# First attention of a two-block transformer forward pass: pairs of heads interleaved as two difference pairs and one MoBA pair, twice per token tile

## The chip, the cores and the metric

The kernel runs on one core of one Trainium2 chip. The metric is the time of one execution on the device in microseconds (us), the median of three runs. Engines are named as in the profile: PE is TensorE (PEld its weight loads), DVE is VectorE, ACT is ScalarE, POOL is GpSimd, SP is SyncE, whose queue fetches the weights.

## The reference

Two small transformer blocks run one after the other over 256 tokens of width 1024, in float32. The change lies in the very first mixer, which computes two kinds of attention from one projection `h = x @ w_in`:

```
def diff_moba_mixer(x, w_in, lam, subln, w_out, lambda_init, rope_d, rope_m):
    h = x @ w_in
    ...
    a = diff_attention(dq, dk, dv, lam, subln, lambda_init)
    b = moba_attention(mq, mk, mv)
    return jnp.concatenate([merge_heads(a), merge_heads(b)], axis=-1) @ w_out
```

Difference attention has 4 heads. Each has two query and key maps of width 64 and one value of width 128; both maps go through a causal softmax and the output weights are `w = p[0] - lam_full * p[1]`. A head's output is then normalized by its root mean square over 128 values and scaled by `subln`. MoBA attention has 4 heads of width 128; with 256 tokens and a block of 256 it comes down to plain causal softmax attention over the one block. Afterwards come layer norms, a squared-ReLU MLP, a gated linear attention, another MLP, and the second block with grouped attention, cross attention, pooling and gated convolutional FFNs.

## The kernel before

Each engine has its own program, written out by hand, and the programs meet only at semaphores. Tokens are handled in two tiles t of 128. Weights come as 207 slabs of 1 MB through a ring of six buffers; ScalarE makes the high part `wh` of a slab (line 586), VectorE the rest `wl` (line 1004), and TensorE multiplies three products of high and low parts.

In the first attention the work is cut into 12 steps, the list `HY_PAIRS` (lines 364 to 366). A step ("pair") is either `("diff", t, h)`, one difference head, whose two maps fill the two halves of a score bank, or `("moba", t, j)`, two MoBA heads. Both put 2 x 128(t+1) scores into one PSUM bank. In the order before, a tile has its four difference pairs first and then its two MoBA pairs. All engines walk through this list in its order:

- TensorE (`attention`, line 2001): for step k it issues the scores of pair k+2 (`scores`, 1920: a bf16 mask matmul on line 1927, then the products on line 1929 for a difference pair and 1939 for a MoBA pair), the transposes of the probabilities of pair k (`probs_T`, 1950, line 1968), and the product with the values of pair k-1 (`values`, 1971, line 1998). Scores of the first two pairs are issued earlier, inside the last chunk of the input projection. The transposes of a difference pair wait for VectorE's `diff_w`, those of a MoBA pair for ScalarE's `exp_done` alone.
- VectorE (`softmax`, 1156): for pair q it takes the maximum of the scores (line 1186) and the scaled bias `nb` (1192), then the after-work `post` of pair q-1. For a difference pair that is a reciprocal, a scaling of the second map and the difference (1165, 1167, 1169). For a MoBA pair it is the copy of the transposed probabilities from PSUM (1178), which waits for `pT_ready`. Behind these, `beside_hy` (1387) puts in, at fixed places, the sums of squares of the first tile's difference heads (k = 4, line 1376), its MoBA output (k = 5, lines 1370 and 1206) and its difference output (k = 7, lines 1383 and 1385), each three pairs after the pair of that number.
- ScalarE (`softmax`, 662): for pair q the two exponentials with row sums (683), then, where pair q-1 is a difference pair, the copy of its transposed weights (672). With pair 6 it also squares the first tile's difference outputs (`diff_squares`, 809, line 811); the squares of the second tile stand behind the loop, and behind them one weight split (line 586) and then the copies of `prep("hy_out")` (593).

The squares of a tile read the PSUM bank that holds all four difference heads of that tile, so `diff_squares(t)` waits on `pv_done`, the count of finished value products, for the last difference pair of the tile. The difference heads of tile 0 go to bank 5, of tile 1 to bank 7; the MoBA heads of both go to bank 6, which the second tile may use once `moba_free` is signalled. Score banks rotate over three, banks for transposes over two.

When the last value product is done, TensorE transposes the first tile of `xn` (line 1646), ScalarE and VectorE make its high and low parts `xhl` (593 and 1017), and the output projection begins (`project_out`, 1685, lines 1706 to 1708). The second tile of `xn` is transposed in the middle of it.

Of the kernel before, what the change touches and what calls it, by code (L numbers as in the profile page):

```python
# [161 lines left out]
def build(nc, d):  # L162
    st, S = plan()
    out = d["out"]
    with ExitStack() as ctx:
# [3 lines left out]
        def sem(name):  # L169
            return ctx.enter_context(nc.semaphore(name))  # L170
# [52 lines left out]
        def ar(col, *dims):  # L223

            n = int(np.prod(dims))
            v = arena[:, col:col + n]
            if len(dims) == 2:
                v = v.rearrange("p (a b) -> p a b", b=dims[1])
            elif len(dims) == 3:
                v = v.rearrange("p (a b c) -> p a b c", b=dims[1], c=dims[2])  # L230
            return v
# [87 lines left out]
        pv_done = sem("pv_done")  # L319
# [43 lines left out]

        HY_PAIRS = []
        for t in range(TT):
            HY_PAIRS += [("diff", t, h) for h in range(4)] + [("moba", t, j) for j in range(2)]
        QK_PAIRS = [("gqa", t, j) for t in range(TT) for j in range(4)]
        XA_PAIRS = [("x", t, j) for j in range(2) for t in range(TT)]
        Q_HY, Q_QK = 0, len(HY_PAIRS)
# [36 lines left out]
        def out_bank(kind, t, j):  # L406

            if kind == "diff":
                return 5 if t == 0 else 7
            if kind == "moba":  # L410
                return 6
            if kind == "gqa":
                return 6 + j // 2
            return 4 + 2 * t + j
# [156 lines left out]
        def _(act):  # L571
# [235 lines left out]
            blocks(0, HY_FILLS, fs=(4, 6))  # L807

            def diff_squares(t):
                act.wait_ge(pv_done, Q_HY + 6 * t + 4)  # L810
                nc.scalar.activation(ar(HY_SQ, TT, CH)[:, t, :], ps[out_bank("diff", t, 0)][:, :], ACT.Square).then_inc(sq_done, 1)

            softmax(HY_PAIRS, Q_HY, lambda k: diff_squares(0) if k == 6 else None, lambda k: copy_nat(5) if k == 1 else None)
            diff_squares(1)
            splits(st["hy_out"], 0, 1)
            prep("hy_out")
# [1544 lines left out]
```

## Time and profile before

| | |
|---|---|
| runs | 1339.33, 1339.55, 1338.05 us; median 1339.33 |
| profiled execution | 1339.7 us |
| its span | 1337.7 us |
| mean granted TensorE clock | 0.996 of full speed |
| busy, share of the span | PE 97%, PEld 84%, DVE 68%, ACT 51%, POOL 7% |
| first attention, first pair's maximum to the output projection's first matmul | 79.22 to 110.35 us |

The span is what the profiler saw from first to last instruction; the time of that execution is 2.0 us longer. A busy share is an average over the whole kernel; in the first attention TensorE is far less busy than 97%. In the timelines a line is one instruction or several alike in a row (the count after x); the end of a TensorE line is modelled and overlaps the next one, so what a matmul costs in a row is read from start to start. The granted clock is 1.00 at 2.4 GHz and 0.50 at 1.2 GHz.

### The profile page before, as it was taken

The page shows a single profiled execution, that of the slowest core. Times are in us where ns is not written, and L with a number is a line of the kernel's source. Part 1 is how long each engine was busy: PE and PEld are TensorE (multiplying, and loading weights), DVE is VectorE, ACT ScalarE, POOL GpSimd, SP SyncE. Part 2 cuts the span into 40 slices and gives each one's busy share as a digit, 9 for nine tenths or more (in the row PEclk, how much of TensorE's full clock was granted, in tenths as well). Part 3 has the DMA queues.
Part 4 walks back from the last instruction along what each step waited for, and adds up shares of the span by engine and source line. Part 5 has one row for each costly group of instructions (what it writes and reads, how often), then busy time and mean ns, then how long its engine had stood idle before and what let it go on. Part 6 is the DMA issues. An engine that isn't in the chain of part 4 may idle for free.

```text
span 1337.7 us, 18077 instructions
## 1 busy us (share of the span) xinstructions
PE 1303.3 (97%) x7247; PEld 1124.6 (84%) x7247; DVE 912.0 (68%) x997; ACT 683.1 (51%) x817; POOL 98.3 (7%) x135
## 2 busy tenths in 40 slices
PE   8989999999999999999999999999999989999997
PEld 6867888888888888888888888888888888788885
DVE  4987766657477865666777655787777545687776
ACT  5653544445644454444646543566665442566663
POOL 3100100001240100000220100000001100000000
PEclk9999999999999999999999999999999999999999
DMA  9722655556443655554650533555557441455540
GB/s 347 288 95 82 235 194 192 188 189 216 170 132 129 219 197 192 194 193 167 250 177 11 219 128 126 186 193 192 191 192 246 158 152 56 173 194 194 193 168 31
DMA packets 36066, 235.57 MB, mean 176 GB/s; under 512 B 4136, under 2 KB 4512, under 8 KB 10016
## 3 DMA queue, kind: packets, MB, share of 16 engines
q1 hardware_dynamic: 30384, 217.07, 45.2%
q0 software_dynamic: 4608, 15.82, 3.7%
q10 hardware_dynamic: 1008, 1.77, 0.4%
q8 instruction: 46, 0.75, 0.2%
q14 instruction: 20, 0.16, 0.0%
HBM read 232.54 MB, written 2.10 MB: 175 GB/s over the span
## 4 chain that ended last, share of the span: by engine, by line
PE 85%; DVE 8%; ACT 3%; DMA 2%; issue 1%; POOL 1%; SPq 0%; POOLq 0%; ACTq 0%; DVEq 0%
PE ps L1799 20%; PE ps L1793 11%; PE ps L1814 7%; PE ps L1816 7%; PE ps L1815 7%; PE ps L1706 3%; PE ps L1708 3%; PE ps L1707 3%; PE ps L1676 2%; PE ps L1678 2%; PE ps L1677 2%; DVE wl L1004 2%; PE ps L1998 2%; PE ps L1772 2%; PE ps L1777 2%; PE ps L1773 2%
## 5 line engine op out<-in xcount | busy, mean ns | idle before, releaser
L1004 DVE TENSOR_TENSOR wl<-raw,wh 128x2048 fp32r<-128x2048 f32 x203 | 463.1, 2289 | 169.8 <-ACT wh L586 169.6
L586 ACT ACTIVATE wh<-raw 128x2048 fp32r<-128x2048 f32 x203 | 386.7, 1908 | 139.1 <-PE ps L1799 77.0
L1799 PE MATMUL ps<-xhl,wh 128*128 128x512 f32 x1216 | 290.1, 391 | 0.0
L1799 PEld LDWEIGHTS ps<-xhl,wh 128*128 128x128 f32 x1216 | 223.5, 188 | 43.2
L1814 PE MATMUL ps<-wh,hh 128*128 128x512 f32 x432 | 168.3, 390 | 2.8 <-DVE hl L1291 2.8
L1815 PE MATMUL ps<-wl,hh 128*128 128x512 f32 x432 | 168.1, 389 | 0.0
L1816 PE MATMUL ps<-wh,hl 128*128 128x512 f32 x432 | 168.1, 389 | 0.0
L1793 PEld LDWEIGHTS ps<-xhl,wl 128*128 128x128 f32 x1216 | 155.9, 191 | 6.0 <-issue 0.6
L1793 PE MATMUL ps<-xhl,wl 128*128 128x256 f32 x1216 | 159.0, 284 | 0.0
L1814 PEld LDWEIGHTS ps<-wh,hh 128*128 128x128 f32 x432 | 81.1, 188 | 20.4 <-DVE hl L1291 3.7
L1816 PEld LDWEIGHTS ps<-wh,hl 128*128 128x128 f32 x432 | 81.1, 188 | 16.9
L1815 PEld LDWEIGHTS ps<-wl,hh 128*128 128x128 f32 x432 | 81.1, 188 | 16.8
L1676 PE MATMUL ps<-wh,xhl 128*128 128x512 f32 x208 | 82.4, 396 | 0.4 <-DVE xhl L1017 0.2
L1677 PE MATMUL ps<-wl,xhl 128*128 128x512 f32 x208 | 81.1, 390 | 0.0
L1678 PE MATMUL ps<-wh,xhl 128*128 128x512 f32 x208 | 81.0, 390 | 0.0
L1269 DVE SCALAR_TENSOR_TENSOR arena<-arena,cw 128x255 f32<-128x255 f32 x88 | 38.8, 481 | 59.7 <-ACT arena L736 59.7
L736 ACT ACTIVATE arena<-arena,cw 128x256 f32<-128x256 f32 x88 | 48.2, 594 | 56.6 <-DVE arena L1263 56.6
L473 POOL TENSOR_SCALAR rstd<-var 128x1 f32<-128x1 f32 (+2 forms) x28 | 11.7, 419 | 822.5 <-ACT arena L641 360.2
L706 ACT ACTIVATE hh<-arena 128x512 fp32r<-128x512 f32 x32 | 20.2, 633 | 98.3 <-DVE arena L1232 98.3
L593 ACT ACTIVATE xhl<-ps 128x512 fp32r<-128x512 f32 x56 | 30.2, 593 | 68.1 <-PE ps L1646 68.1
L1706 PE MATMUL ps<-wh,xhl 128*128 128x512 f32 x160 | 63.2, 395 | 1.5 <-DVE xhl L1017 1.5
L1017 DVE TENSOR_TENSOR xhl<-ps,xhl 128x512 fp32r<-128x512 f32 x56 | 35.9, 684 | 40.6 <-ACT xhl L593 40.6
(256 smaller groups left out, 1950.4 us busy)
## 6 DMA issues: line engine op xcount, KB each, us to landing
raw<-in_w_slabs SPq DMA_DIRECT2D x203, 1024.0 KB, 4.8
raw<-in_w_slabs SPq DMA_DIRECT2D x4, 512.0 KB, 8.2
X<-in_x SPq DMA_DIRECT2D x2, 512.0 KB, 5.6
qk<-in_mem POOLq DMA_DIRECT2D x1, 1024.0 KB, 14.7
gains<-in_mem_norm POOLq DMA_DIRECT2D x2, 512.0 KB, 10.8
gains<-in_ln_mix_g POOLq DMA_DIRECT2D x2, 512.0 KB, 14.0
gains<-in_ln_mix_b POOLq DMA_DIRECT2D x2, 512.0 KB, 7.5
gains<-in_ln_ffn_g POOLq DMA_DIRECT2D x2, 512.0 KB, 4.6
```

Source lines behind the costliest of these rows:

```text
L586: nc.scalar.activation(wh[:, s % RING, :], raw[:, s % LOWS, :], ACT.Copy).then_inc(wh_ready, 1)
L736: ins = nc.scalar.activation(dst[:, a, :], u[:, part, a, :], ACT.Identity, scale=cw[:, l, 1, bass.ds(f, 1)], bias=cw[:, l, 3, bass.ds(f, 1)])
L1004: nc.vector.tensor_tensor(wl[:, s % LOWS, :], raw[:, s % LOWS, :], wh[:, s % RING, :].bitcast(F32), ALU.subtract)\
L1676: nc.tensor.matmul(o, x[0][:, kt, ts], wa[:, k, :], start=(kt == 0), stop=False)
L1677: nc.tensor.matmul(o, x[0][:, kt, ts], wb[:, k, :], start=False, stop=False)
L1678: ins = nc.tensor.matmul(o, x[1][:, kt, ts], wa[:, k, :], start=False, stop=(kt == KT - 1))
L1706: nc.tensor.matmul(o, xh[:, kt, ts], wa[:, k, :], start=(kt == 0), stop=False)
L1793: nc.tensor.matmul(ps[bank + a][:, 0:T], wb[:, kt, a * P:(a + 1) * P], xh[:, kt, :], start=(kt == 0), stop=False, skip_group_check=True)
L1799: ins = nc.tensor.matmul(ps[bank + a], wa[:, kt, a * P:(a + 1) * P], xhl[:, kt, :, :], start=False, stop=(kt == KT - 1), skip_group_check= ...
L1814: nc.tensor.matmul(o, hh[:, par, k, ts], wa[:, k, cs], start=False, stop=False, skip_group_check=True)
L1815: nc.tensor.matmul(o, hh[:, par, k, ts], wb[:, k, cs], start=False, stop=False, skip_group_check=True)
L1816: ins = nc.tensor.matmul(o, hl[:, par, k, ts], wa[:, k, cs], start=False, stop=last and k == 1, skip_group_check=True)
```

## The change

In each token tile the order of the six pairs becomes two difference pairs, one MoBA pair, two difference pairs, one MoBA pair. Since the last difference pair of a tile is now the fifth pair and no longer the fourth, the squares wait for five finished value products of the tile instead of four. No instruction is added or taken away, and the places of the side work on VectorE and ScalarE stay the same.

```
         for t in range(TT):
-            HY_PAIRS += [("diff", t, h) for h in range(4)] + [("moba", t, j) for j in range(2)]
+            for j in range(2):
+                HY_PAIRS += [("diff", t, 2 * j), ("diff", t, 2 * j + 1), ("moba", t, j)]
...
             def diff_squares(t):
-                act.wait_ge(pv_done, Q_HY + 6 * t + 4)
+                act.wait_ge(pv_done, Q_HY + 6 * t + 5)
```

## Rows read from the trace of the kernel before

**Rows 1.** The page's chain that ended last, shares by engine

```profile
PE 85%; DVE 8%; ACT 3%; DMA 2%; issue 1%; POOL 1%; SPq 0%; POOLq 0%; ACTq 0%; DVEq 0%
```

**Rows 2.** Windows; after the times and length: PE, PEld, DVE, ACT, POOL, PEclk, DMA

```profile
83.50:86.70 3.20, 1.41 (x8) 0.86 (x7) 1.40 (x6) 1.97 (x7) 0.00 (x0) 1.00 0.60 205
86.90:90.10 3.20, 3.20 (x16) 3.03 (x15) 2.33 (x10) 2.00 (x10) 0.00 (x0) 0.50 0.22 92
...
103.70:106.90 3.20, 1.79 (x17) 1.60 (x16) 1.97 (x5) 2.17 (x6) 0.00 (x0) 1.00 0.02 5
```

**Rows 3.** Timeline of VectorE, first token tile: start, duration, line, tiles, [idle before]

```profile
85.19 0.42 DVE L1186 TENSOR_REDUCE mx<-ps 128x2 f32<-128x256 f32 x1 [1.79 <-PE ps L1929]
...
86.57 0.42 DVE L1186 TENSOR_REDUCE mx<-ps 128x2 f32<-128x256 f32 x1
...
87.68 0.35 DVE L1169 SCALAR_TENSOR_TENSOR arena<-arena,rr 128x128 f32<-128x128 f32 x1
88.68 0.42 DVE L1186 TENSOR_REDUCE mx<-ps 128x2 f32<-128x256 f32 x1 [0.66 <-PE ps L1939]
...
91.98 0.42 DVE L1178 COPY arena<-ps 128x256 f32<-128x256 f32 x1 [0.98 <-PE ps L1968]
92.33 0.68 DVE L1186 TENSOR_REDUCE mx<-ps 128x2 f32<-128x512 f32 x1
...
93.39 0.42 DVE L1178 COPY arena<-ps 128x256 f32<-128x256 f32 x1 [0.19 <-PE ps L1968]
```

**Rows 4.** Timeline of VectorE, second token tile

```profile
98.01 0.17 DVE L1370 RECIPROCAL rr<-rs 128x4 f32<-128x4 f32 x1
...
98.82 0.68 DVE L1186 TENSOR_REDUCE mx<-ps 128x2 f32<-128x512 f32 x1
...
100.25 0.48 DVE L1169 SCALAR_TENSOR_TENSOR arena<-arena,rr 128x256 f32<-128x256 f32 x1
100.65 0.68 DVE L1186 TENSOR_REDUCE mx<-ps 128x2 f32<-128x512 f32 x1
...
106.50 0.69 DVE L1178 COPY arena<-ps 128x512 f32<-128x512 f32 x1 [1.20 <-PE ps L1968]
```

**Rows 5.** Timeline of TensorE, both tiles and the output projection's start

```profile
86.71 0.44 PE L1968 MATMUL ps<-con,arena 128*128 128x128 f32 x1 [0.90 <-DVE arena L1169]
...
87.37 0.42 PE L1927 MATMUL ps<-bfc 128*128 128x256 bf16 x1
...
88.44 0.42 PE L1968 MATMUL ps<-con,arena 128*128 128x128 f32 x1
...
90.70 1.02 PE L1929 MATMUL ps<-qk 128*128 128x512 f32 x2
91.56 0.38 PE L1968 MATMUL ps<-con,arena 128*128 128x128 f32 x2
...
95.71 0.44 PE L1968 MATMUL ps<-con,arena 128*128 128x128 f32 x2 [0.94 <-DVE arena L1169]
95.98 0.61 PE L1998 MATMUL ps<-arena 128*128 128x128 f32 x4
...
96.54 1.02 PE L1929 MATMUL ps<-xn,qk 128*128 128x512 f32 x2
...
105.81 0.65 PE L1968 MATMUL ps<-con,arena 128*128 128x128 f32 x4 [1.41 <-ACT arena L683]
...
110.35 0.47 PE L1706 MATMUL ps<-wh,xhl 128*128 128x512 f32 x1 [1.07 <-DVE xhl L1017]
...
118.64 0.60 PE L1646 MATMUL ps<-con,xn 128*128 128x128 f32 x4
```

**Rows 6.** Timeline of ScalarE, behind the last pair

```profile
105.65 0.59 ACT L811 ACTIVATE arena<-ps 128x512 f32<-128x512 f32 x1
106.12 1.92 ACT L586 ACTIVATE wh<-raw 128x2048 fp32r<-128x2048 f32 x1
108.88 1.08 ACT L593 ACTIVATE xhl<-ps 128x512 fp32r<-128x512 f32 x2 [0.84 <-PE ps L1646]
```

## The prediction, made blind

> **What bounds the kernel now.** I read the page first. TensorE carries 85% of the chain that ended last, VectorE 8% [rows 1]: nearly everywhere the time is that of matmuls in a row, and a VectorE or ScalarE delay costs only where TensorE has run out of other work. The first attention is such a place, since no weight slab is multiplied in it. I then read the timelines of the three engines from 79 to 119 us, by pair. I number the pairs 0 to 11 in program order and write S, T and V for TensorE's scores, transposes and values of a pair, exp for ScalarE's exponentials, and "copy" for the move of the transposed MoBA probabilities, which VectorE does; ScalarE does it for a difference pair.
>
> Two rules of order decide. TensorE goes S(q+2), T(q), V(q-1). VectorE goes max(q+1), bias(q+1), then the after-work of pair q: for a difference pair reciprocal and two products, T waiting for them; for a MoBA pair the copy, which itself waits for T. So a MoBA copy stops VectorE until TensorE has come to T(q), and max(q+2) stands behind it.
>
> In the first tile an after-work of a difference pair ends 1.46 us after its max starts, the next max can start after 1.38 [rows 3]; the order before loses 0.66 to wait for S(4) and then 0.98 and 0.19 before the two copies [rows 3]. From 92 us on VectorE has no gap until the last copy, before which it waits 1.20 [rows 4]. TensorE's clock is 1.2 GHz in the stretch 86.9 to 90.1 and 2.4 GHz before and after; just before it fell, TensorE had been busy 1.41 of 3.2 us [rows 2].
>
> **The change by parts.** It adds and removes no instruction: 12 pairs, the same shapes. It moves MoBA pair 4 to place 2 and pair 10 to place 8; places 5 and 11 stay MoBA. The squares of a tile wait for five values instead of four. I replay the places with the durations of the rows, a consumer starting 0.04 to 0.06 us after its source, as in every handover here.
>
> Places 0 and 1 are the same, so is all to T(1) at 86.71 [rows 5]. Place 2 is MoBA now. After bias(3), at 87.10, VectorE stands at copy(2). T(2) is behind S(4) on TensorE, and the clock is low. S(4) took 1.07 there, from its mask at 87.37 to T(2) at 88.44, as a MoBA pair [rows 5]; as a difference pair it has two matmuls of 256 columns for four of 128, so the same. T(2) starts at 88.44 again, but its two transposes (0.44 for a slow one, the second 0.21 behind) land only at 89.07 and copy(2) runs at 89.11. max follows a copy by 0.35 [rows 3]: max(4) at 89.46, where it was at 88.68: 0.78 late. Its after-work gives T(3) at 90.98. V(2) has two heads now, four instructions in place of two, 0.45 as from V(5) at 95.98 to the next mask, in place of 0.22. So S(6) begins at 91.60, 1.0 later than before (90.59, its bf16 mask being 0.11 ahead of the row). A second-tile S takes 0.97 from its mask to the T behind it [rows 5], T(4) and V(3) 0.17 and 0.22, S(7) 0.97 again: T(5) 93.93, copy(5) 94.35 against 93.39 [rows 3]. From there to T(6) both orders do the same: 96.66 against 95.71 [rows 5]. **First tile: 0.95 late.** Were the clock high all through, both orders would be quicker and the same replay gives 95.62 against 94.97, 0.65 late: these are the two ends of this term, and I take the first, as the row shows the low clock.
>
> Second tile. A difference pair costs VectorE 1.83 from max to max [rows 4]. max(8) is at 97.13 (after the sums of squares, about 0.6, which stand in both orders), bias(8) 97.84, the products of pair 7 end at 99.04, the MoBA output takes 0.81 [rows 4], max(9) is at 99.78, and at 100.57 VectorE comes to copy(8). TensorE: T(7) 99.10, V(6), S(10) until 100.79, and only then the four transposes of T(8), landing 0.65 later, as the last ones do [rows 4, 5]: copy(8) at 101.45. **VectorE idles 0.88**, which the order before has not. Before, places 6 to 9 are four difference pairs in a row and place 10 is a MoBA pair whose T has no scores ahead of it.
>
> Then max(10) 102.06, products of pair 9 end 103.97, output of the first tile's difference heads 1.33, max(11) 105.23, bias(11) ends 106.11. Now the other half of the exchange: place 10 is a difference pair, its products end at 107.14, T(10) is at 107.20. V(9) 0.45. T(11), which before started as soon as its exponentials had ended, at 105.81 [rows 5], is behind both: 107.92. copy(11) 108.61, against 106.50 [rows 4]: **2.11 late**. As work, VectorE does the same between 86.57 and this copy, so 2.11 is just the sum of its added waits.
>
> **The tail** adds a little. The squares of the second tile wait for V(10), not V(9). Before, ScalarE ran them at 105.65 without a wait, and the weight split behind them was over before the transposes of the output projection were ready at 108.88 [rows 6]. Now V(10) lands at 109.02, the squares run at 109.06, the split queued behind them at 109.53, and the copy of xhl behind the split can start 1.84 later, at 111.37, though its transposes are ready at 111.0. So 111.37 against 108.88, **2.49 late**, of which 0.38 is this queue. If the split ends hidden, 2.11 stays; that is the lower end. The sums of squares, POOL's power and the second tile's output are wanted only at the second prep, at 118.64 + 2.5 [rows 5], hence hidden: they begin after the squares at 109.65 and end by about 115.5; without that cover they would cost their own 2.5 us. No DMA moves: the weight ring is full and is not read in this stage.
>
> Nothing afterwards takes the delay back: the output projection's first matmul (110.35) [rows 5], and all behind it, hang on that xhl.
>
> **The clock in the tail.** In this order TensorE has nothing to do between S(11)'s end at about 102.95 and T(9) at 104.03, and from V(8)'s end at 105.45 to T(10) at 107.20: gaps of 1.08 and 1.75 with 1.4 of work between. Before its fall at 86.8 it had 1.41 of work in 3.2 us, and as its last wait was 0.90, none of the waits there was longer than that [rows 2, 5]. In the order before, the stretch 103.7 to 106.9 had 1.79 us of work in 3.2 and kept 2.4 GHz [rows 2]. The new stretch is emptier than the one after which the clock fell, so I take it that it falls again, about 107 to 109, for as long as the row shows (3.4 us). V(9) is then 0.85, T(11) 0.87 to issue, V(10) lands at 110.45; squares, split: xhl at 112.81 instead of 111.37. **1.44 us.** Ends: nothing if it does not fall, 1.7 us (half of 3.4) if all of the slow stretch is matmuls that are waited for.
>
> The Trainium skill (TensorE: Matmul & The Clock Gate, "HAM oscillation") warns of idle gaps longer than any that stand here, before or after; by that rule this term would be nothing and the sum 1341.8. The trace speaks against it: the clock fell at 86.8 after gaps of 0.9. A later paragraph of the page, on a second failure mode, has short gaps that come often enough lower the clock too; by it the sum is 1343.3.
>
> Sum: 2.49 + 1.44 = 3.9. The profiled execution took 1339.7 us (span 1337.7, 2.0 around it), 0.4 above the median 1339.33; on the median this gives 1343.2. The two terms by their own ends, against the median: 2.1 - 0.3 (the first tile warm) = 1.8 to 2.5 + 1.7 = 4.2, plus the runs' spread of 1.5 us. 0.2% is 2.7 us here, about what a measurement can tell from no change.
>
> **The rivals.**
> B, the clock holds in the tail: 1341.8, +2.5, just inside 0.2%. For it: the gap of 1.41 before 105.81 did nothing. Against: the stretch with that gap still held 1.79 of work, here it is 1.4 in more time.
> C, the waits are partly absorbed: TensorE comes to T(2) and T(8) earlier than I place them, say because S(4) and S(10) hardly delay them, and the split in the tail stays hidden. T(8) ahead of S(10) would take 0.88 away, the split 0.38: +1.2, 1340.6. Against: TensorE runs in program order and S is ahead of T in every group of the timeline.
> D, faster: interleaving fills VectorE's waits before copies instead of making them. If VectorE met both first-tile copies with T already done, 0.98 and 0.19 would go, and 0.66 with an earlier S(4): -1.8 and, with a shorter tail wait (1.20 before the last copy), -3.0: 1336.3. It decides at copy(2): T(2) would have to be done at 87.10, and S(4) ends only at 88.4. Almost excluded by the order on TensorE.
>
> **Chances.** Both terms (1343.2) 0.50, B 0.28, C 0.15, D 0.05, something slower than all 0.02. Slower by over 0.2% takes the first but for a tenth, a quarter of B (spread of the runs) and the last: 0.54. Faster 0.06, the same 0.40. Range: from C to the first case's upper end and the spread, 1340.3 to 1344.8; the likeliest case alone, 1342.3 to 1344.5.
>
> **What would show it.** VectorE idle of about 2.0 before copy(2), 0.8 before copy(5), 0.9 before copy(8), 1.5 before copy(11); the transposes T(8) start right after S(10); T(6) near 96.7; first matmul of the output projection near 112.9 with the clock high and 114.3 with it low; in ScalarE the squares of the second tile 1.9 us after the last exponentials, and the split right behind them; the granted clock 0.50 somewhere after 106. I am wrong if the copies find their T done, if the low clock of 86.8 is not there or there are more such stretches, or if a later stage takes the delay back.

## The result, and the profile after

The changed kernel takes 1344.38 us (median of 22 executions, 1338.35 to 1354.73), the kernel before 1339.21 (22, 1336.59 to 1348.33). The medians differ by 5.2 us; the ratio of the two is estimated at 1.0041 with a 95% interval of 1.0024 to 1.0058, which is 5.5 us more (3.2 to 7.8). 3.9 were forecast. The profiled execution of the changed kernel took 1344.91 us, span 1343.1, 5.4 us over the span before. Line numbers are one higher than before.

VectorE, its four copies of MoBA probabilities (places 2, 5, 8, 11; compare [rows 3, 4]):

```profile
88.53 0.42 DVE L1179 COPY arena<-ps 128x256 f32<-128x256 f32 x1 [0.87 <-PE ps L1969]
...
93.69 0.42 DVE L1179 COPY arena<-ps 128x256 f32<-128x256 f32 x1 [0.63 <-PE ps L1969]
...
100.77 0.69 DVE L1179 COPY arena<-ps 128x512 f32<-128x512 f32 x1 [0.78 <-PE ps L1969]
...
108.95 0.69 DVE L1179 COPY arena<-ps 128x512 f32<-128x512 f32 x1 [2.49 <-PE ps L1969]
```

TensorE: S(2) from its mask, T(6), T(8), T(9), T(10), T(11), the output projection's first matmul (compare [rows 5]):

```profile
84.90 0.28 PE L1928 MATMUL ps<-bfc 128*128 128x256 bf16 x1 [0.91 <-ACT arena L603]
...
96.00 0.44 PE L1969 MATMUL ps<-con,arena 128*128 128x128 f32 x2 [1.16 <-DVE arena L1170]
...
100.13 0.60 PE L1969 MATMUL ps<-con,arena 128*128 128x128 f32 x4
...
103.35 0.44 PE L1969 MATMUL ps<-con,arena 128*128 128x128 f32 x2 [1.20 <-DVE arena L1170]
...
106.51 0.69 PE L1969 MATMUL ps<-con,arena 128*128 128x128 f32 x2 [1.83 <-DVE arena L1170]
...
107.85 1.06 PE L1969 MATMUL ps<-con,arena 128*128 128x128 f32 x4
...
114.12 0.47 PE L1707 MATMUL ps<-wh,xhl 128*128 128x512 f32 x1 [1.07 <-DVE xhl L1018]
```

ScalarE behind the last pair (compare [rows 6]):

```profile
109.80 0.60 ACT L812 ACTIVATE arena<-ps 128x512 f32<-128x512 f32 x1 [2.18 <-PE ps L1999]
110.30 1.90 ACT L587 ACTIVATE wh<-raw 128x2048 fp32r<-128x2048 f32 x1
112.66 1.08 ACT L594 ACTIVATE xhl<-ps 128x512 fp32r<-128x512 f32 x2 [0.46 <-PE ps L1647]
```

Windows of the changed kernel, columns as in [rows 2]:

```profile
86.90:90.10 3.20, 2.09 (x15) 1.78 (x15) 2.19 (x9) 1.78 (x10) 0.00 (x0) 1.00 0.38 161
102.10:105.30 3.20, 1.38 (x11) 1.14 (x10) 3.06 (x8) 1.41 (x5) 0.00 (x0) 1.00 0.03 5
105.70:112.40 6.70, 5.89 (x26) 5.66 (x27) 2.10 (x4) 3.56 (x7) 1.11 (x2) 0.50 0.00 0
709.90:716.50 6.60, 6.60 (x32) 5.66 (x31) 1.59 (x2) 1.79 (x8) 0.00 (x0) 0.50 0.01 2
```

All four copies now wait, 0.87, 0.63, 0.78 and 2.49 us (the last also by the low clock), and T(8) starts 0.86 after the first product of S(10), right behind it. The clock is high in the first tile this time and low from 105.7 to 112.4, so T(10), T(11) and the values behind them run at half speed. TensorE waits 1.20 and 1.83 us before T(9) and T(10). ScalarE's squares come 2.2 us after its last copy, and its split ends before the transposes are ready.

To take the start of the stage out of the comparison I measure from the mask of S(2). The output projection's first matmul is 29.22 us behind it (114.12 - 84.90); in the trace before it was 25.91 (110.35 - 84.44, the mask of S(2) being at 84.44). So the stage costs 3.3 us between the two traces. The rest of the difference of the two spans can be followed by the same ScalarE instruction in both traces. This execution was 0.5 us late at S(2) already. A ScalarE copy just ahead of the long waits of the grouped attention (line 632, now 633) is at 699.71 before and at 703.48 after: 3.8 us late, as at the projection, so nothing in 590 us takes the delay back. Behind the grouped attention a weight split (line 586, now 587) is at 729.51 and at 736.39: 6.9 us late, since this trace has a low clock there, at 709.9 to 716.5, which the trace before has not. And a copy (line 606, now 607) at 1098.74 is at 1104.14: 5.4 us late, since the trace before has a low clock at 1073.2 to 1076.6 and this one has not. 0.5 + 3.3 + 3.1 - 1.5 is the 5.4 us between the spans.

**The spread is the clock's.** In the 22 executions of the changed kernel time follows the mean granted clock: 1338.35 and 1338.48 us at 0.998, 1343.05 to 1345.85 at 0.993 or 0.994, 1353.45 to 1354.73 at 0.986 to 0.988. A straight line through the 22 has 1.3 us for 0.001 of mean clock. So one must ask of the change both what it makes TensorE wait for and when the clock is low.

### The profile page after: what moved, and what is told of

It is laid out like the page before. It is cut to its first block, busy times and chain, and to the rows that moved or that the text cites. A ratio compares the mean times of both kernels' runs of the same rounds, so it can differ in the third digit from the quotient of the medians.

```text
span 1343.1 us, 18077 instructions
## 1 busy us (share of the span) xinstructions
PE 1307.1 (97%) x7247; PEld 1127.8 (84%) x7247; DVE 912.4 (68%) x997; ACT 683.3 (51%) x817; POOL 98.3 (7%) x135
## 4 chain that ended last, share of the span: by engine, by line
PE 85%; DVE 8%; ACT 3%; DMA 2%; issue 1%; POOL 1%; POOLq 0%; ACTq 0%; DVEq 0%
PE ps L1800 20%; PE ps L1794 11%; PE ps L1815 7%; PE ps L1817 7%; PE ps L1816 7%; PE ps L1707 3%; PE ps L1709 3%; PE ps L1708 3%; PE ps L1677 3%; PE ps L1679 3%; PE ps L1678 3%; DVE wl L1005 2%; PE ps L1999 2%; PE ps L1773 2%; PE ps L1778 2%; PE ps L1774 2%
## 6 DMA issues: line engine op xcount, KB each, us to landing
gains<-in_mem_norm POOLq DMA_DIRECT2D x2, 512.0 KB, 11.1
```

## The experiments

Each is compared at the same points; "mean" is over its timed executions, with its standard error. Over all executions run beside the experiments the kernel before has a mean of 1340.3 +- 0.3 us (104; its first 22 have 1340.3 too), the changed kernel, its first 22 and 12 more, 1345.0 +- 0.8 (34). The experiments ran on four chips, on which the kernel before has means from 1339.3 to 1341.1; e1 to e4 shared one chip, e5 to e8 another, e9 and e10 a third. A trace is of one execution.

**e1 and e2: one tile each.** The new order in tile 0 alone, in tile 1 alone; the squares wait for 5 there, for 4 in the other tile. The edits are against the kernel before.

```
-            HY_PAIRS += [("diff", t, h) for h in range(4)] + [("moba", t, j) for j in range(2)]
+            if t == 0:      # e2: t == 1
+                for j in range(2):
+                    HY_PAIRS += [("diff", t, 2 * j), ("diff", t, 2 * j + 1), ("moba", t, j)]
+            else:
+                HY_PAIRS += [("diff", t, h) for h in range(4)] + [("moba", t, j) for j in range(2)]
...
-                act.wait_ge(pv_done, Q_HY + 6 * t + 4)
+                act.wait_ge(pv_done, Q_HY + 6 * t + (5 if t == 0 else 4))      # e2: t == 1
```

> Only the first token tile has the new order; the second keeps four difference pairs and then two MoBA pairs. Theory A (waits before the MoBA copies, plus a low clock that follows from an empty stretch at place 9 and 10): the first tile costs 0.65 us (clock high in it) to 0.95 us (clock low), seen as T(6) later by that, measured from S(2); the second tile then goes as in the kernel before, with one wait of about 1.2 us before copy(11), and the clock stays high from T(6) to the output projection: 0.7 to 1.0 us in all. Theory B (the whole loss is the clock's): T(6) not later than before at the same clock, total within 0.3 us. Theory C (every MoBA pair between difference pairs costs the same): half of the whole loss, about 1.6 us at the output projection's first matmul.

> Only the second token tile has the new order. Theory A: T(6) as in the kernel before, VectorE idle about 0.8 us before copy(8) and 1.5 us or more before copy(11); the empty stretch before T(10) is there, so the clock falls in the tail in nearly every execution: copy(11) 1.2 us late, the output projection's first matmul 1.5 us late at a high clock and 2.5 to 4 us late with the low one. Theory B: the same fall and its 2 us, but without the low clock nothing. Theory C: about 1.6 us.

TensorE in e1, then in e2: mask of S(2), T(6), first matmul of the projection.

```profile
84.83 0.28 PE L1931 MATMUL ps<-bfc 128*128 128x256 bf16 x1 [0.89 <-ACT arena L606]
...
95.94 0.44 PE L1972 MATMUL ps<-con,arena 128*128 128x128 f32 x2 [1.16 <-DVE arena L1173]
...
110.58 0.47 PE L1710 MATMUL ps<-wh,xhl 128*128 128x512 f32 x1 [1.07 <-DVE xhl L1021]
```

```profile
83.90 0.28 PE L1931 MATMUL ps<-bfc 128*128 128x256 bf16 x1 [0.89 <-ACT arena L606]
...
94.42 0.44 PE L1972 MATMUL ps<-con,arena 128*128 128x128 f32 x2 [0.93 <-DVE arena L1173]
...
110.49 0.47 PE L1710 MATMUL ps<-wh,xhl 128*128 128x512 f32 x1 [1.42 <-DVE xhl L1021]
```

VectorE in e2, the last two copies (places 8 and 11):

```profile
99.18 0.69 DVE L1182 COPY arena<-ps 128x512 f32<-128x512 f32 x1 [0.77 <-PE ps L1972]
...
106.29 0.69 DVE L1182 COPY arena<-ps 128x512 f32<-128x512 f32 x1 [1.42 <-PE ps L1972]
```

Neither trace has a low clock in this stage. From S(2), e1 has T(6) after 11.11 us and the projection after 25.75; e2 after 10.52 and 26.59. The kernel before at a high clock (e4, below) has 10.52 and 25.17. So tile 0 costs 0.59 at T(6) and 0.58 at the end, tile 1 costs 1.42. Theory A has the places right and its sizes come out a little too large (0.65 and 0.7 to 1.0 for e1, 1.5 for e2). B falls, since the waits cost this at a high clock, and C falls by e1, where 1.6 was to be. But the low clock that A expected in nearly every execution of e2 is missing here, with TensorE's waits of 1.20 before T(9) and 1.84 before T(10) in place. Timed: e1 1.0007 (0.9980 to 1.0034), e2 1.0025 (0.9997 to 1.0052), too wide to add to that.

**e3 and e4: TensorE kept busy.** Dummy matmuls on zeros in front of its waits, in the changed kernel and in the one before (the table for e4 is 1: 3, 6: 3, 7: 1, 8: 2, 11: 5). For the dummies before S(2) the wait for the blocks is moved ahead of the wait for the bank.

```
                 p = ar(pbuf(kind)[0], 2, 2, T)[:, q % 2]
+                if kind in ("diff", "moba"):
+                    stay_warm({1: 3, 3: 4, 6: 4, 7: 1, 9: 4, 10: 7}.get(q, 0), 3 + q % 2)
...
+            blocks_done(0, HY_FILLS)
+            stay_warm(3, 7)
             pe.wait_ge(bank_free, st["hy_in"].f0 + 4 + 12)
-            blocks_done(0, HY_FILLS)
```

> The changed kernel with dummy bf16 matmuls on zeros (0.22 us each) put in front of TensorE's waits, into the PSUM bank that the next transposes overwrite: 3 before S(2), 3, 4, 4, 1, 4 and 7 before T(1), T(3), T(6), T(7), T(9), T(10). Theory A: the clock stays at 2.4 GHz to the output projection; the waits of VectorE stay (0.9 before copy(2), 0.6 before copy(5), 0.8 before copy(8), 1.5 before copy(11)), and from S(2) to the projection's first matmul it takes about 28.0 us: 2.1 more than the kernel before in its trace, 2.9 more than that with a high clock throughout, and 1.2 or more less than the changed kernel with its low clock. Theory B (all of it is the clock): within 0.3 us of the kernel before.

> The kernel before with the same dummies where it waits: 3 before S(2), 3, 3, 1, 2 and 5 before T(1), T(6), T(7), T(8), T(11). Theory A: the low clock at 86.8 us goes, and with it 0.7 us: S(2) to the projection's first matmul 25.2 instead of 25.9 us, and in time some 0.5 to 1 us less than the kernel before. Theory B says the same; if the dummies cost something themselves (a rival of the method), it takes 25.9 us or more.

TensorE in e3, mask of S(2), then from the scores of place 11 on:

```profile
85.13 0.28 PE L1928 MATMUL ps<-bfc 128*128 128x256 bf16 x1 [0.25 <-ACT arena L603]
...
102.22 1.03 PE L1654 MATMUL ps<-zero_bf 128*128 128x512 bf16 x4
103.58 0.44 PE L1971 MATMUL ps<-con,arena 128*128 128x128 f32 x2 [0.34 <-DVE arena L1170]
...
104.96 1.46 PE L1654 MATMUL ps<-zero_bf 128*128 128x512 bf16 x6
106.75 0.44 PE L1971 MATMUL ps<-con,arena 128*128 128x128 f32 x2 [0.33 <-DVE arena L1170]
...
112.31 0.47 PE L1707 MATMUL ps<-wh,xhl 128*128 128x512 f32 x1 [1.42 <-DVE xhl L1018]
```

TensorE in e4, mask of S(2), T(6), projection:

```profile
84.75 0.28 PE L1927 MATMUL ps<-bfc 128*128 128x256 bf16 x1 [0.23 <-ACT arena L602]
...
95.27 0.44 PE L1970 MATMUL ps<-con,arena 128*128 128x128 f32 x2 [0.29 <-DVE arena L1169]
...
109.92 0.47 PE L1706 MATMUL ps<-wh,xhl 128*128 128x512 f32 x1 [1.07 <-DVE xhl L1017]
```

At a high clock throughout the stage takes 27.18 us in the new order and 25.17 in the old: **the waits alone cost 2.01 us**, and e1's 0.58 and e2's 1.42 add up to it. Theory B is out. Theory A's size was too large: about 28.0 us were expected, 2.9 more than the kernel before at a high clock. The dummies fit into the waits: e10 (the kernel before) and e9 (the changed one) below have none in this stage and a high clock, and take 25.18 and 27.18 us. TensorE in e10, then in e9, mask of S(2) and first matmul of the projection:

```profile
83.78 0.28 PE L1927 MATMUL ps<-bfc 128*128 128x256 bf16 x1 [0.91 <-ACT arena L602]
...
108.96 0.47 PE L1706 MATMUL ps<-wh,xhl 128*128 128x512 f32 x1 [1.07 <-DVE xhl L1017]
```

```profile
84.30 0.28 PE L1928 MATMUL ps<-bfc 128*128 128x256 bf16 x1 [0.91 <-ACT arena L603]
...
111.48 0.47 PE L1707 MATMUL ps<-wh,xhl 128*128 128x512 f32 x1 [1.42 <-DVE xhl L1018]
```

VectorE's copies of MoBA probabilities that wait in e10, places 4, 5 and 11 (the one of place 10 does not):

```profile
90.58 0.42 DVE L1178 COPY arena<-ps 128x256 f32<-128x256 f32 x1 [1.29 <-PE ps L1970]
91.99 0.42 DVE L1178 COPY arena<-ps 128x256 f32<-128x256 f32 x1 [0.18 <-PE ps L1970]
...
105.11 0.69 DVE L1178 COPY arena<-ps 128x512 f32<-128x512 f32 x1 [1.20 <-PE ps L1970]
```

So at a high clock the old order has waits before its copies too, 2.7 us of them. In the new order they are 0.87, 0.62, 0.77 and 1.41 us (e9), with 0.47 more before a maximum of scores: 4.1 us. Both also wait 1.80 before the maximum of S(2). The two copies of the first tile together wait as long as before (1.49 against 1.47 us); those of the second tile 2.18 against 1.20.

The two traces' difference of 3.3 us is now resolved: the old order lost 0.74 to its low clock at 86.8 (25.91 - 25.17), the new one 2.04 to its own (29.22 - 27.18). (Of the 7 dummies before T(10) the trace has recorded 6.) Timed, e3 is 1341.7 +- 0.6 us, ratio 1.0006 (0.9984 to 1.0029), and e4 1340.9 +- 0.8, ratio 1.0003 (0.9984 to 1.0021): the 0.5 to 1 us less that was expected of e4 does not show in times, nor do the 2.01 us between e3 and e4 (0.8 +- 1.0). Its own trace says why so few executions don't resolve it: it has a low clock of 17.1 us from 705.5 on, in the grouped attention, and loses 8.0 us there against the trace of the kernel before.

**e5: transposes ahead of scores for MoBA pairs.**

```
+                    early = pair[0] == "moba"
+                    if early:
+                        probs_T(q0 + k, *pair)
                     if a < len(pairs):
                         scores(q0 + a, a % n, *pairs[a])
...
-                    probs_T(q0 + k, *pair)
+                    if not early:
+                        probs_T(q0 + k, *pair)
```

> The changed kernel, but TensorE issues the transposes of a MoBA pair before the scores of the pair two places on, not behind them. Theory A (VectorE stands at a MoBA copy because T is behind S): copy(2), copy(5) and copy(8) come 0.5, 1.0 and 1.5 us earlier after S(2) than in the changed kernel, the wait before copy(8) is gone, T(6) is 10.4 us after S(2) instead of 11.1, and at a high clock the projection's first matmul is 25.9 us after S(2) instead of 27.2: 0.7 more than the kernel before at a high clock; in time about 1.3 us less than the changed kernel. Rival (the after-work of the pairs, not the order on TensorE, sets the pace): copies earlier, T(6) and the projection not, 27.2 us.

VectorE's copies (the mask of S(2) is at 83.77 in this trace):

```profile
86.87 0.42 DVE L1179 COPY arena<-ps 128x256 f32<-128x256 f32 x1 [0.33 <-PE ps L1969]
...
91.51 0.42 DVE L1179 COPY arena<-ps 128x256 f32<-128x256 f32 x1
...
98.12 0.69 DVE L1179 COPY arena<-ps 128x512 f32<-128x512 f32 x1
...
106.56 0.69 DVE L1179 COPY arena<-ps 128x512 f32<-128x512 f32 x1 [2.49 <-PE ps L1969]
```

After S(2) they are at 3.10, 7.74 and 14.35 us; in the changed kernel 3.63, 8.79 and 15.87. The waits before places 5 and 8 are gone. max(11) is 1.26 us earlier, T(6) at 10.45. The end could not be read at a high clock: this execution has a low one from 103.8 to 107.2, and the projection comes after 27.37, so the 25.9 of theory A is open. What decides is there though: the copies waited because T stood behind S, and T(6) came earlier with them, against the rival. Timed, e5 has 1340.9 +- 1.0 us, ratio to the kernel before 1.0003 (0.9985 to 1.0021); on the same chip the changed kernel (e7) has 1344.8 +- 1.4. That is 3.8 +- 1.7 us less where 1.3 were expected, and part of it can be the clock in later stages.

**e6: the split ahead of the squares in the tail.**

```
-            diff_squares(1)
             splits(st["hy_out"], 0, 1)
+            diff_squares(1)
```

> The changed kernel, but in the tail ScalarE makes the weight split before the squares of the second tile, so the copy of xhl does not queue behind squares and split. If the queue costs 0.38 us as forecast: 26.8 us from S(2) to the projection's first matmul at a high clock, and nothing if the clock is low in the tail, since TensorE's transposes are then the later ones (29.2 us as in the changed kernel's trace). Rival (the queue hides nothing and costs nothing): 27.2 us. The clock: low somewhere between 105 and 113 us.

ScalarE: split, squares, copy of xhl.

```profile
107.18 1.90 ACT L587 ACTIVATE wh<-raw 128x2048 fp32r<-128x2048 f32 x1
109.46 0.60 ACT L812 ACTIVATE arena<-ps 128x512 f32<-128x512 f32 x1 [0.38 <-PE ps L1999]
112.20 1.09 ACT L594 ACTIVATE xhl<-ps 128x512 fp32r<-128x512 f32 x2 [2.14 <-PE ps L1647]
```

The clock is low from 105.1 to 111.9, and the copy of xhl waits 2.14 us for TensorE though the split was over long before: 29.11 us from S(2), against 29.22 and, in e7's trace, 29.04. With a low clock this queue costs nothing. (e6 was executed once, 1353.92 us; its trace has a low clock at 709.2 to 733.1 as well.) At a high one it does: in e2 copy(11) is 1.07 us late after S(2) and the copy of xhl 1.43, a difference of 0.36 against the forecast's 0.38.

**e7: the changed kernel again.**

> The changed kernel itself in further executions. If the low clock in the tail follows from the empty stretch before T(9) and T(10): its trace shows it again between 104 and 113 us, and the mean granted clock over its executions lies some 0.002 to 0.003 under that of the kernel before. If the one in the first trace was an accident: no low clock there, and equal mean clocks.

Windows of this trace, columns as in [rows 2]:

```profile
105.40:112.00 6.60, 5.50 (x25) 5.28 (x26) 2.35 (x6) 3.62 (x7) 0.73 (x2) 0.50 0.00 0
709.60:733.20 23.60, 23.60 (x108) 20.77 (x107) 9.46 (x12) 7.72 (x29) 0.00 (x0) 0.50 0.00 1
```

The low clock in the tail is there again, and one of 23.9 us in the grouped attention. Timed: 1.0031 (1.0011 to 1.0052), mean clock 0.9937 against 0.9965 of the kernel before beside it, the 0.002 to 0.003 that were expected. But the mean clock takes in the grouped attention too, so for the tail only the trace counts.

**e9, e10, e11: what is the rest of the 5 us?** The changed kernel's executions above 1346 us are 11 of 34, those of the kernel before 8 of 104 (12 of 126 with its first 22). e9 and e10 put dummies into two waits of the grouped attention (1.56 and 1.82 us in the first trace of the changed kernel), of the changed kernel and of the one before; e11 has the line of e3 with `{9: 4, 10: 7}` alone.

```
             blocks_done(8, QK_FILLS)
+            stay_warm(6, 6)
             pe.wait_ge(fill_done, 8)
...
+                if q == Q_QK + 1:
+                    stay_warm(7, 6)
```

> The changed kernel with dummies only in TensorE's two long waits at the grouped attention (6 before its second scores, 7 before its second transposes), none in the first attention. Open is why the changed kernel's median moved by 5 us when the first attention shows 3.3 to 4.1. Theory A (the first attention costs 4, and the rest is the low clock at the grouped attention, which some executions have and others not): no execution above 1346 us, mean 1.5 to 3 us under the changed kernel's 1345.0, and 3.5 to 4 us above e10. Rival (the spread has another source): the executions above 1346 us stay, mean 1344 to 1346.

> The kernel before with the same dummies at the grouped attention only. Theory A: no execution above 1346 us, mean 1338 to 1339.5 us (the kernel before has 1340.5), and e9 is 3.5 to 4 us above it. Rival: mean 1340 to 1341, and e9 is 4.5 to 5.5 us above it.

> The changed kernel with dummies only before T(9) and T(10) (4 and 7), the two waits of the second tile that the new order brings; nothing at the grouped attention. Open is whether the long low-clock stretch at the grouped attention (executions above 1346 us: 11 of 34 of the changed kernel, 8 of 87 of the one before) goes with the low clock in the tail. Linked: with the tail fed at most 1 of 12 executions is above 1346 us, mean 1341 to 1342.5. Independent of it: 3 to 5 of 12 are, mean 1343.5 to 1345. In both its trace has no low clock in the tail, and 27.2 us from S(2) to the projection's first matmul if the first tile is at a high clock.

Windows of e9:

```profile
103.00:105.00 2.00, 1.08 (x10) 0.89 (x8) 1.89 (x6) 0.52 (x2) 0.00 (x0) 1.00 0.04 8
105.20:111.80 6.60, 4.12 (x32) 3.68 (x33) 3.17 (x6) 4.44 (x9) 1.21 (x2) 1.00 0.00 0
```

e9: 1341.0 +- 0.4 us, ratio to the kernel before 1.0000 (0.9982 to 1.0018); e10: 1338.6 +- 0.2, ratio 0.9992 (0.9980 to 1.0004). None of their 24 executions is above 1346 (the highest 1343.05 and 1340.73). The long executions are the low clock of the grouped attention: all four traces of executions above 1346 us have a long one there. In e4, then in e6:

```profile
705.60:722.50 16.90, 16.90 (x79) 15.02 (x76) 6.60 (x9) 6.00 (x23) 0.00 (x0) 0.50 0.00 0
```

```profile
709.40:733.00 23.60, 23.60 (x107) 20.78 (x106) 9.53 (x12) 7.75 (x29) 0.00 (x0) 0.50 0.00 1
```

e7 is shown above, and e5 has 10.2 us from 707.9 on. By the same instructions of ScalarE as in the section on the result, they lose 4.8 (e5), 8.0 (e4) and 11.1 us (e6, e7) there. With the low clock there gone, the change costs 2.4 +- 0.5 us (e9 less e10, same chip), below the 3.5 to 4 of theory A; and e9's trace has the same waits before T(9) and T(10), 1.20 and 1.84 us, with the clock high in the whole stage: 27.18 us. The low clock in the tail comes in some executions only. The grouped attention then accounts for 2.3 of the 4.7 us between the means, within about 1 us: its dummies take 4.1 us off the changed kernel's mean and 1.7 off that of the one before. The changed kernel itself was not timed on that chip, so the 4.1 is between chips.

e11 has no low clock in the tail, 27.16 us, 3 of 12 executions above 1346, a mean of 1342.6 +- 1.2 and a ratio of 1.0025 (1.0004 to 1.0045). By the count the two are independent; the mean lies in neither expectation. With e3, which also feeds these two waits, it is 4 of 24, and so few executions can't tell the two cases apart. That the grouped attention can have its low clock without one in the tail is seen in e4. Yet the traces without dummies at the grouped attention lean the other way: all four with a low clock in the tail (the changed kernel twice, e5, e6) have one in the grouped attention, of the six without (before, e1 to e4, e11) one has. e3 and e7 reach it at the same time of their traces, the copy on line 633 being at 703.26 us in both; e3, its tail fed, keeps the high clock, e7 has the 23.9 us. Whether the two are linked stays open.

**e8: the old order, mended.** MoBA transposes ahead of scores as in e5, the dummies of e4 (2 instead of 3 before T(6)) and those of e10.

> The order of the kernel before with MoBA transposes ahead of scores and with dummy matmuls in TensorE's waits of the first attention (3 before S(2); 3, 2, 1, 2, 5 before T(1), T(6), T(7), T(8), T(11)) and in its two long waits at the grouped attention (6 before its second scores, 7 before its second transposes). Theory A: copy(4) and copy(5) 1.0 and 0.6 us earlier, T(6) 0.3 us earlier than the fed kernel before, 24.8 us from S(2) to the projection; no low clock there nor near 705 us, so that the executions of 1347 us and more disappear and the mean falls by 1.5 to 3 us against the kernel before. Rival: the low clock has other causes than these waits, the mean stays within 1 us.

TensorE: mask of S(2), T(6), projection.

```profile
84.80 0.28 PE L1927 MATMUL ps<-bfc 128*128 128x256 bf16 x1 [0.25 <-ACT arena L602]
...
94.99 0.44 PE L1972 MATMUL ps<-con,arena 128*128 128x128 f32 x2 [0.18 <-DVE arena L1169]
...
109.64 0.47 PE L1706 MATMUL ps<-wh,xhl 128*128 128x512 f32 x1 [1.07 <-DVE xhl L1017]
```

24.84 us from S(2), 0.33 below e4, T(6) 0.33 earlier, copy(4) and copy(5) 0.96 and 0.60 earlier, as expected of theory A; no low clock before the last matmul. 1337.5 +- 0.4 us, the highest of 12 at 1340.48, ratio to the kernel before 0.9984 (0.9972 to 0.9996). It has the lowest mean of all versions, 2.8 us below the kernel before over all chips (2.3 on its own, where 1.5 to 3 were expected). How much of it is the order on TensorE and how much the dummies was not separated in time; in the stage the order gives 0.33 us.

## Why the prediction came out as it did

**VectorE stands at a MoBA copy because T is behind S: right.** The first tile was forecast at 0.65 late with a high clock and measured 0.59. Before copy(2) VectorE was to wait 2.0 us; it waits 0.87, the clock being high there. Before copy(8) VectorE waits 0.78 (forecast 0.88), T(8) starts right behind S(10), and e5 removes that wait. The second tile up to copy(11) was forecast at 1.16 (2.11 less 0.95) and is 1.07 in e2.

At a high clock the three terms of the forecast add up to 2.19 us (0.65, 1.16 and 0.38), and 2.01 were measured.

**The tail's queue of squares and split: right at a high clock** (0.36 against 0.38), and it vanishes at a low one (e6). The prediction added its 1.44 of low clock on top of the ScalarE chain; in the trace TensorE itself was last.

**The clock in the tail: right that it falls, wrong in how often and how long.** The forecast took 3.4 us of low clock and 1.44 of cost; the trace has 6.8 and 2.04. It fell at 105.7, before T(10), within the wait. That it falls is no certainty. Of the six traces with the new order in tile 1 and nothing added to TensorE's waits there, four have the low clock (the changed kernel twice, e5, e6), and two, e2 and e9, have not, with the same waits of 1.20 and 1.84 us as the changed kernel. The two with these waits fed (e3, e11) have a high clock, which is too few to show that the waits are the cause; it stays open. The rule of the Trainium skill (TensorE: Matmul & The Clock Gate, "HAM oscillation") that warns of longer idle gaps than these would have kept the clock high, and the traces speak against it: waits of 1.20 and 1.83 us stood ahead of the fall. The page's "A second HAM failure mode", in which short waits that come often enough let the clock go up and down (in another kernel), is nearer to them, but does not say why e2 and e9 kept it high.

**The first tile: the forecast took the low clock at 86.8 us for a property of the kernel before.** It is not there in e10's trace of the same instructions in this stage, nor in e2's, whose first tile is the old one. "The low clock of 86.8 is not there or there are more such stretches" was one of the forecast's own signs of being wrong, and both came true. So 0.95 was the term for one execution, and 0.59 is what the order costs.

**"Nothing afterwards takes the delay back": right, but something afterwards adds to it.** This is the step that was missing: the forecast put every later stage at nothing. The range's upper end, 1344.8, held by 0.4 us (its own terms, 4.2 above the median and 1.5 of spread, add up to 1345.0). The grouped attention, 600 us later and untouched by the change, has a low clock more often in the changed kernel. 2.3 of the 4.7 us of mean are there, within about 1 us. Why more often is open: the change shifts the arrival there by 2 to 4 us, and its low clock in the tail may be linked with it or not (e11); an experiment that only shifts the arrival was not made.

**The number owes something to luck.** The first attention was forecast at 3.9 us and costs 2.01, or about 4.0 in an execution with the low clock in the tail, less 0.74 where the kernel before has its own. With the grouped attention fed the whole change is 2.4 us, where rival B was forecast. That the median lies in the range, and within the likeliest case's 1342.3 to 1344.5, is owed to some 2 us from a stage that the forecast left out.

Rivals C (waits absorbed) and D (interleaving fills waits) are out: T(8) stands right behind S(10), no copy of the new order finds its transposes done, and VectorE's waits up to copy(11) grow from 2.7 to 4.1 us (e10, e9). B (high clock in the tail, +2.5) is what an execution such as e9's shows, at 2.0.

## What to carry to other kernels

Where an engine walks through mixed work in order, put side by side what the other engines do next: here a copy that waits for transposes costs most when the transposes stand behind the scores of a later pair, and issuing those transposes first took 1.3 us off the new order up to its last copy (e5) and 0.33 off the old one (e8). Alternating kinds of work evens nothing out if each alternation adds a wait at the head of a queue. Where the clock is low in some executions and not in others, compare a stage between traces of equal clock, and read the mean clock beside each time before believing a difference of half a per cent.

## What the runs showed of the hardware

The same instructions with the same waits ran with the clock at 1.2 GHz for 6.8 us in one execution (29.2 us for the stage) and at 2.4 GHz in another (27.2; e9). In the grouped attention a low clock once begun lasted 6.8 us in one trace of the changed kernel and 23.9 us in another, TensorE busy all the while. With 13 dummy matmuls of 0.22 us in two waits there the kernel before had a mean of 1338.6 us and a highest execution of 1340.7 (12); without them, on the same chip, 1340.3 and 1348.5 (23).
